# Latent query products: the rank of 448 cut as three row tiles of 128 and a stacked rest of 64, in place of four tiles of 112

## What is computed

```python
cq, ckv, k_rope, z = jnp.split(h @ w_in, [448, 960, 1024], axis=-1)
q = (rms_norm(cq, q_norm_g) @ w_uq).reshape(B, S, 16, 128 + 64)
kv = (rms_norm(ckv, kv_norm_g) @ w_ukv).reshape(B, S, 16, 128 + 128)
# rotary embedding on q_rope and k_rope, chunk-causal softmax, values
y = o.reshape(B, S, 2048) * jax.nn.silu(z)
return y @ w_out
```

## Time and profile before

| | us |
|---|---|
| median of 3 runs | 2478.34 (2477.54 to 2480.36) |
| the profiled execution | 2477.93, its span 2476.1 |
| PE busy | 2433.2 (98% of the span) |
| VectorE busy | 1889.0 (76%) |
| ScalarE busy | 1399.4 (57%) |
| GpSimd busy | 442.0 (18%) |
| granted TensorE clock, mean | 0.999 of full speed |

### The profile page before, as it was taken

The page is one execution under the profiler, slowest core; times in us unless marked ns, Lnnn a source line. Parts: engine busy times, 40 slices in busy tenths (PEclk is TensorE's granted clock), DMA queues, the critical chain, the costliest instruction groups (busy, mean ns, idle before and its releaser), DMA issues.

```text
span 2476.1 us, 31108 instructions
## 1 busy us (share of the span) xinstructions
PE 2433.2 (98%) x11597; PEld 2018.7 (82%) x11597; DVE 1889.0 (76%) x2295; ACT 1399.4 (57%) x1934; POOL 442.0 (18%) x298
## 2 busy tenths in 40 slices
PE   6999999999999999998999999999999999999999
PEld 5888888888887989887888888888888888888887
DVE  7899798977777787866655555557988878788884
ACT  6655765444447555555566676755655545555553
POOL 0264563111020000110000000043111021111111
PEclk9999999999999999999999999999999999999999
DMA  9999677978784877754555556455465555646454
GB/s 364 321 341 349 237 256 273 336 283 290 271 313 149 246 212 220 233 208 149 167 173 163 177 153 183 157 187 187 155 236 170 204 187 191 217 170 221 170 203 154
DMA packets 370999, 549.47 MB, mean 222 GB/s; under 512 B 31405, under 2 KB 158129, under 8 KB 370225
## 3 DMA queue, kind: packets, MB, share of 16 engines
q1 hardware_dynamic: 368688, 539.54, 64.6%
q10 hardware_dynamic: 1824, 6.04, 0.7%
q0 software_dynamic: 352, 2.11, 0.2%
HBM read 545.53 MB, written 2.11 MB: 221 GB/s over the span
## 4 chain that ended last, share of the span: by engine, by line
PE 88%; DVE 8%; ACT 2%; issue 1%; DMA 1%; SPq 0%; POOL 0%; DVEq 0%; ACTq 0%; POOLq 0%
PE ps L2393 48%; PE ps L2398 24%; DVE lo L1305 3%; PE ps L2423 2%; PE ps L2419 2%; PE ps L2420 2%; DVE ps L1330 1%; PE ps L2379 1%; PE ps L2378 1%; PE ps L2380 1%; DVE lo L1282 1%; DMA raw<-in_sgu_w_in 1%; PE ps L3007 1%; PE ps L2655 1%; ACT hi L630 1%
## 5 line engine op out<-in xcount | busy, mean ns | idle before, releaser
L1305 DVE TENSOR_TENSOR lo<-raw,hi 128x1024 fp32r<-128x1024 f32 x550 | 706.9, 1304 | 350.8 <-ACT hi L630 350.2
L630 ACT ACTIVATE hi<-raw 128x1024 fp32r<-128x1024 f32 x550 | 571.3, 1051 | 431.3 <-PE ps L2398 352.7
L2393 PE MATMUL ps<-hi,a_hi 128*128 128x512 f32 (+1 forms) x2016 | 798.6, 396 | 2.1 <-issue 0.9
L2393 PE MATMUL ps<-hi,a_lo 128*128 128x512 f32 (+1 forms) x2016 | 785.6, 390 | 0.0
L2398 PE MATMUL ps<-lo,a_hi 128*128 128x512 f32 (+1 forms) x2016 | 539.0, 389 | 1.5 <-DVE lo L1305 1.5
L616 ACT ACTIVATE hi<-raw 128x1024 fp32r<-128x1024 f32 x339 | 358.2, 1060 | 292.7 <-PE ps L2398 255.2
L1282 DVE TENSOR_TENSOR lo<-raw,hi 128x1024 fp32r<-128x1024 f32 x339 | 424.4, 1272 | 107.2 <-ACT hi L616 105.0
L2393 PEld LDWEIGHTS ps<-hi,a_hi 128*128 128x128 f32 x2016 | 378.7, 188 | 85.1 <-issue 5.3
L2398 PEld LDWEIGHTS ps<-lo,a_hi 128*128 128x128 f32 x2016 | 378.4, 188 | 81.1 <-DVE lo L1305 1.9
L2393 PEld LDWEIGHTS ps<-hi,a_lo 128*128 128x128 f32 x2016 | 378.9, 188 | 74.4
L2393 PE MATMUL ps<-hi,b_hi 128*128 128x512 f32 x880 | 347.4, 395 | 0.6 <-ACT y L1015 0.3
(11 more groups left out here) (351 smaller groups left out, 2436.6 us busy)
## 6 DMA issues: line engine op xcount, KB each, us to landing
raw<-in_sgu_w_in SPq DMA_DIRECT2D x88, 1024.0 KB
raw<-in_ada_w SPq DMA_DIRECT2D x64, 1024.0 KB
raw<-in_w_up SPq DMA_DIRECT2D x64, 1024.0 KB
raw<-in_w_down SPq DMA_DIRECT2D x64, 1024.0 KB
raw<-in_w_in SPq DMA_DIRECT2D x42, 1024.0 KB
raw<-in_ada_w SPq DMA_DIRECT2D x64, 512.0 KB
raw<-in_sgu_w_out SPq DMA_DIRECT2D x32, 1024.0 KB
raw<-in_w_in SPq DMA_DIRECT2D x128, 256.0 KB
```

The source lines that it names most:

```text
L630: nc.scalar.activation(hi[:, q % CHUNKS, 0:width], raw[:, r % RAWS, q % 2 * CW:q % 2 * CW + width], ACT.Copy).then_inc(hi_ready, 1)
L1305: nc.vector.tensor_tensor(lo[:, q % CHUNKS, 0:width], raw[:, r % RAWS, q % 2 * CW:q % 2 * CW + width], hi[:, q % CHUNKS, 0:width].bitcast( ...
L2393: nc.tensor.matmul(ps[:, 2 * s + t, 0:width], x[:, k0 + j, t * P:(t + 1) * P], hi[:, c, w], start=begins, stop=False)
```

## The change

The latent query is cut as three tiles of 128 rows and a rest of 64. The rest stands twice in tile 3: rows 0 to 63 of `b_hi` hold its high part, rows 64 to 127 its low part, and the weights' rest is loaded twice too, into both halves of the rows. One product of 128 rows with the weights' high part then gives two of the three terms, and a product of 64 rows, weights' low part by query's high part, the third: 3 x 3 + 2 = 11 products per output. For this VectorE writes the last 64 scaled columns twice, a fifth split operation goes to rows 64 to 127 of `b_hi`, the gain's rest is loaded twice, and an even head's weights come in 12 transfers, an odd head's in 3. `LAND` goes from 96 to 224 so that a slab can be divided into that many parts.

```diff
-LAND = 96
+LAND = 224
@@ the small vectors, SP
-                (rb[B_QG:B_QG + 4, 0:112], d["mla_q_norm_g"].rearrange("a (r q) -> (a r) q", q=112)),
+                (rb[B_QG:B_QG + 3, :], d["mla_q_norm_g"][:, 0:384].rearrange("a (r q) -> (a r) q", q=P)),
+                (rb[B_QG + 3:B_QG + 4, 0:64], d["mla_q_norm_g"][:, 384:448]),
+                (rb[B_QG + 3:B_QG + 4, 64:P], d["mla_q_norm_g"][:, 384:448]),
@@ head_parts, SP
-                    place = lambda c0, c1: lambda s: s[0:112, e * CW:(e + 1) * CW].rearrange("p (k n) -> p k n", k=4)[:, :, c0:c1]
-                    q0 = i * 192
+                    q0, wide = i * 192, P if i % 2 else S
+                    rows = lambda s, p0, p1, k0, k1: s[p0:p1, e * CW + k0 * wide:e * CW + k1 * wide]
+
+                    def placed(cut, source):
+                        return [(lambda s: cut(rows(s, 0, P, 0, 3).rearrange("p (k n) -> p k n", k=3)), source(uq_tiles))] + [
+                            (lambda s, p=p: cut(rows(s, p, p + 64, 3, 4).rearrange("p (k n) -> p k n", k=1)),
+                             source(uq_rest.rearrange("p (k n) -> p k n", k=1))) for p in (0, 64)]
+
                     if i % 2:
-                        return [(lambda s: s[0:112, e * CW:e * CW + NB].rearrange("p (k n) -> p k n", k=4), uq[:, :, q0:q0 + P])]
-                    return [(place(c, c + w), uq[:, :, q0 + q:q0 + q + w]) for c, w, q in
-                            ((0, 160, 0), (160, 32, 320), (192, 32, 160), (224, 32, 352))]
+                        return placed(lambda a: a, lambda w: w[:, :, q0:q0 + P])
+                    return placed(lambda a: a[:, :, 0:160], lambda w: w[:, :, q0:q0 + 160]) + placed(
+                        lambda a: a[:, :, 192:224], lambda w: w[:, :, q0 + 160:q0 + 192]) + placed(
+                        lambda a: a[:, :, 160:192], lambda w: w[:, :, q0 + 320:q0 + 352]) + placed(
+                        lambda a: a[:, :, 224:256], lambda w: w[:, :, q0 + 352:q0 + 384])
@@ ScalarE
-            act_split(act, n, 2, b_hi, 112, scale=lambda k: vb[0:112, B_QG + k:B_QG + k + 1], fresh=True)
+            act_split(act, n, 2, b_hi, scale=lambda k: vb[:, B_QG + k:B_QG + k + 1], fresh=True)
@@ VectorE
+        def dve_split_query(dve, n):
+
+            for g in range(2):
+                dve.wait_ge(t_hi, n.tg.base + 1)
+                for e in range(2):
+                    k = 2 * g + e
+                    for rows, to in ((slice(0, 64), b_lo), (slice(64, P), b_hi)) if k == 3 else ((slice(0, P), b_lo),):
+                        ins = nc.vector.scalar_tensor_tensor(out=to[rows, k, :], in0=ps[rows, 4 + n.tg.base % 2, e * S:(e + 1) * S],
+                                                             scalar=vb[rows, B_QG + k:B_QG + k + 1], in1=b_hi[rows, k, :].bitcast(F32),
+                                                             op0=ALU.mult, op1=ALU.subtract)
+                ins.then_inc(t_lo, 1)
+                n.tg.base += 1
@@
             dve_norm(dve, n, 448)
             for t in range(T):
+                nc.vector.tensor_scalar(v[:, t, D + 448:D + 512], cq[t][:, 384:448], rstd[:, t:t + 1], None, ALU.mult).then_inc(c_ready, 1)
+            dve.wait_ge(c_ready, 4)
+            for t in range(T):
                 nc.vector.tensor_scalar(cq[t], cq[t], rstd[:, t:t + 1], None, ALU.mult).then_inc(c_ready, 1)
@@
-            dve_split(dve, n, 2, b_hi, b_lo, 112, scale=lambda k: vb[0:112, B_QG + k:B_QG + k + 1])
+            dve_split_query(dve, n)
@@ PE
-            pe.wait_ge(small_landed, 128)
+            pe.wait_ge(small_landed, 160)
@@ query, PE
-                    for k in range(4):
+                    for k in range(3):
                         w = slice(k * step + q, k * step + q + P)
-                        ins = three(o, b_hi[0:112, k, :], b_lo[0:112, k, :], hi[0:112, c, w], lo[0:112, c, w], k == 0, k == 3, True)
+                        three(o, b_hi[:, k, :], b_lo[:, k, :], hi[:, c, w], lo[:, c, w], k == 0, False, True)
+                    w = slice(3 * step + q, 3 * step + q + P)
+                    mm(o, hi[:, c, w], b_hi[:, 3, :], start=False, stop=False)
+                    ins = mm(o, lo[0:64, c, w], b_hi[0:64, 3, :], start=False, stop=True)
@@
-            latent(4, lambda t, k: v[:, t, D + 112 * k:D + 112 * (k + 1)], 112)
+            latent(6, cols(v, D))
```

More of the change, by code:

```diff
@@ L530, in _ @@
                            LAND - 48 if q == 3 else 16) for q in range(4)))
-            uq = d["mla_w_uq"][0].rearrange("(k p) n -> p k n", p=112)
+            uq = d["mla_w_uq"][0]
+            uq_tiles = uq[0:3 * P, :].rearrange("(k p) n -> p k n", p=P)
+            uq_rest = uq[3 * P:448, :]
             ukv = d["mla_w_ukv"][0].rearrange("(k p) n -> p k n", p=P)
```

## The result

The changed kernel takes 2487.58 us (median of 8 runs, 2484.54 to 2490.19), the kernel before, run beside it on the same chip, 2480.61 (8 runs, 2477.54 to 2481.77): a ratio of 1.0027, 95% interval 1.0018 to 1.0037. It is slower, by 7.0 us. The profiled execution took 2487.03 us with a span of 2485.2; that of before had 2476.1, so between the two profiles lie 9.1 us.

A forecast was written before the change was run, and what follows sets the result against it. PE (TensorE) was taken to bound the kernel, with 88% of the chain. Profiled 2477.93 us + 6.0 for PE in the head loop + 0.75 for the opening, with the 0.4 to the median, gave 2485.0 us; range 2477.0 to 2488.0.

The forecast's parts named there:

- the base: Starting time of the forecast: the profiled execution's 2477.93 us, plus 0.4 because it lay that far below the median.
- The products removed: Head loop, latent query: 24 of 288 products go, 0.12 us each, 2.9 us less PE work.
- The 64-row product: Eleventh product of each output: going into 64 rows and out costs PE 0.40 us, bounded by 0 and 0.45.
- The first rival: The 64-row product costs no switch; half the saving is lost to VectorE's full stretches: 2477.6 us, chance 0.20.
- its half: The array must be freed but the 64-row product's weight load stays hidden, +0.08 us per output: 2480.3 us, chance 0.04.
- What PE's waits absorb: Heads 0, 4, 8, 12: PE's waits for the exponential hide 0.7 of 6.7 us, leaving +6.0 on the path.
- SP's queue: Head loop: 80 more weight transfers, even slabs issued 3.0 to 4.3 us later, landing 0.5 to 1.4 later; cost 0.
- PE's waits in heads 4, 8 and 12 gone: Sign expected in the changed trace: PE no longer waits for the exponential (L1032) in these heads.
- The second rival: The whole 3.8 us of later issue reaches the slabs of heads 6, 10, 14: 5.7 on top, 2490.7 us, chance 0.08.
- VectorE and ScalarE: Latent query: fifth split operation +0.41 us, norm scalings at most +0.8, ScalarE's extra rows free; nothing reaches PE.
- The opening: Kernel start: two more small-load issues on SP, ahead of ada_w's second slab, add 0.75 us that nothing makes up.
- The clock: Third rival: later PE loses or gains a lower-clock piece worth 3.5 us: 2481.5 or 2488.5 us, chance 0.04.

The follow-up runs named there:

- e1: The changed kernel with the eleventh product at all 128 rows in place of 64: 2481.84 us, ratio to before 1.0004.
- e2: The kernel before with only the last of an output's twelve products at 64 rows in place of 112: 2489.99 us, ratio 1.0034.
- e4: The changed kernel with the two 64-row products of an even head side by side (second form; the first gave no time): 2486.44 us, ratio 1.0020.
- e9: The changed kernel, 64-row product kept, with query weights loaded as before in 4 transfers and 1: 2487.91 us, ratio 1.0020.
- e8: The kernel before, unchanged, profiled once more as a control: 2482.66 us, ratio 1.0005.
- e12: The changed kernel with the eleventh product at 128 rows and the weights' rest loaded once (8 transfers and 2): 2480.69 us, ratio 0.9999.
- e5: The changed kernel with the eleventh product at 128 rows and query weights loaded as before (4 transfers and 1): 2481.58 us, ratio 0.9996.
- e11: As e10, and all nine small loads of the opening from ScalarE's queue: 2482.38 us, ratio to before 1.0004.
- e10: The changed kernel, eleventh product at 128 rows, both rest copies by one transfer (8 and 2), gain loaded from ScalarE's queue: 2481.97 us, ratio 1.0001.
- e6: The kernel before with the query norm's gain loaded in three pieces in place of one: 2481.41 us, ratio 0.9999.
- e3: The changed kernel with the eleventh product at 96 rows in place of 64: 2482.22 us, ratio to before 1.0007.
- e7: The kernel before with query weights in 12 transfers (even heads) and 3 (odd) in place of 4 and 1, products unchanged: 2482.05 us, ratio 1.0003.

## Why the prediction was right, and where it wasn't

**Forecast and base.** 2485.0 us was said and 2487.58 measured, inside the range, slower as said. The difference was put at 6.7 us over the median shown, and 7.0 was measured. 2.3 of the 2.6 us of the miss are the base: the three runs shown had a median of 2478.34, later ones of the same kernel 2480.6 to 2481.8.

**The products removed** cost 0.12 us each, as said; 24 are gone.

**The 64-row product** costs 0.38 us in and out per output, against 0.40 from the attention scores of the second block. The mechanism read there, time until the array is free and a weight load that nothing hides, is what the timeline of after shows (the 64-row product starts 0.09 us late and the next one 0.19, each with its load beside it, and the one after that 0.10), and it carries over to products of the other precision with one half of the rows. e1 and e2 show it from both sides, e4 that it is the step that costs. Per output it is + 0.26 and not + 0.28. The first rival (2477.6) fell with e1 and e2, and its half too.

**What PE's waits absorb** was put at 0.7 us. In e9, with the loads of before, the loop has 21 x 0.26 = 5.46 us more PE work and is 5.04 longer: 0.4 absorbed; ahead of it 3 x 0.26 = 0.78 and 0.47 longer: 0.3. Together 0.7, and e9's trace has no wait for the exponential left. So 24 outputs at + 0.26 less the 0.7 are 5.5 us on the path, where + 6.0 was said.

**SP's queue** was put at nothing; it is 1.0 us (e9 against after). This is the mis-sized term, and it made up for the 0.5 above; that the forecast came so near is in this part luck. The step that failed is the length of the later issue: at 0.32 to 0.5 us a transfer it was 3.0 to 4.3 us; the twelve took 8.15 us in place of 2.18, 6.0 more. Of the 5.2 us behind the last issue, in which it was to lie, 1.4 are still there in after, so only 3.8 of the 6.0 were covered. Counted from the first issue, ScalarE got the slabs of heads 6, 10 and 14 2.1, 1.8 and 2.8 us later than before, and not 0.5 to 1.4; in hand were 1.1 and, with PE slower, 0.8 more. PE's waits come in the same order: 0.1 us in head 4, none in head 8, 0.4 in head 12, so that "PE's waits in heads 4, 8 and 12 gone" holds for head 8 alone. ScalarE's waits are 1.7 us longer per slab than in before, 1.2 than in e8. The second rival's mechanism was at work, at a sixth of its price of 5.7. e12 shows that the reasoning as such holds up to 5.5 us of issue.

**VectorE and ScalarE** at nothing: in e1, e5 and e11, which have the fifth split and the second scaling, the stretch to turn 0 is 112.47 to 112.48 us, as in the control's 112.48.

**The opening** at + 0.75: the mean start of the first product moved by 0.67. That nothing behind makes it up wasn't shown. If all of it reaches the end, the parts are 5.5 + 1.0 + 0.7 = 7.2 us, where the medians differ by 7.0; medians of this kernel can't tell that from 6.5. The reason given, the second slab issued later, can't be the whole of it, since e11 issues that slab 4 us earlier and gains nothing.

**The saving that can't be had.** The first rival said that without a row step only half of the 2.9 us would come out, 1.4, since VectorE sets the end in heads 0, 4, 8 and 12. e5 and e12 have just that, 1.5 us in the loop, the first with the weights' old transfers and the second without the second copy of their rest. So even with transfers that cost nothing this change is worth less than what a measurement of this kernel can tell.

**The clock** rival: after had a piece at the lower level that before had not, worth 1.1 us in that one profile (114.08 against e9's 112.95). Two variants with the eleventh product at 128 rows (e10, e12) had such a piece too, and e9, with 64 rows, had none there, so it isn't the change's alone. The price of the rival was too high. The piece behind the head loop lasts 6.8 us in before and 3.4 in e6 and e12 (granted clock 0.97 between 1100 and 1150 us), but their last stretch of the table isn't shorter by 1.7 us: 1438.23 and 1438.43, against 1438.29 and 1438.40. PE is busy for only 41.32 of the 50 us there, so it doesn't set the time.

## What to carry to other kernels

One product fewer isn't a gain if one of those left steps down to 64 rows: the step into 64 rows and out costs as much as three of these 256-column products. Either give that product all the rows, if what it then adds does no harm, or put the 64-row products of several outputs side by side, which pays the step once. Before counting a saving on PE, look which engine sets the end in each part of the loop, and before splitting a load, compare the time in which the queue issues a whole slab with the time in hand; and judge edits of one stage by marks inside the profile, which here repeated to 0.1 us while whole runs of one kernel scatter by 4 to 10.

## What the runs showed of the hardware

Of the row counts tried, 64 costs a step between products with 128 rows, and 96 doesn't (e3). The Trainium skill, TensorEngine Tiling (Array Packing), Key Properties, says that a change of the tiling mode drains the TensorE, which fits 0.38 us at 64 rows and nothing at 96. It isn't the rows alone: in the kernel before, products with 128 rows and weights of 64 columns (L2916, 128*64) cost a step too. The chain there:

```profile
1217.27 0.81 PE ps L2916 x12
1218.07 2.04 PE ps L2393 x8
```

The block of eight behind them takes 2.04 us, as behind 64 rows (2.05), and not 1.83 as behind transposes of 128 by 128.

The scatter of this kernel isn't spread over the run: against before, ScalarE's high parts shift only in the first 335 us, and from there to the 251st (738 us in before) each variant keeps its distance or comes back to it. One source is at the very start. The first products of 512 columns in before:

```profile
29.51 0.47 PE L2393 MATMUL ps<-hi,a_hi 128*128 128x512 f32 x1 [0.94 <-issue]
29.81 0.39 PE L2393 MATMUL ps<-hi,a_lo 128*128 128x512 f32 x1
```

and in e8_control, the same kernel:

```profile
29.77 0.77 PE L2393 MATMUL ps<-hi,a_hi 128*128 128x512 f32 x1 [0.95 <-issue]
30.34 0.63 PE L2393 MATMUL ps<-hi,a_lo 128*128 128x512 f32 x1
30.76 0.63 PE L2393 MATMUL ps<-hi,a_hi 128*128 128x512 f32 x1
```

In the second the products last 0.63 us and start 0.42 apart, and not 0.39 and 0.23. The granted clock of the profile is 1.00 there in both kernels (29.5 to 34 us). But the pace is that of the piece near 780 us in after, where the granted clock is at the lower of its two levels (1.2 GHz; 0.62 of full speed in the window at the end, which holds 3.4 us of it):

```profile
782.29 0.63 PE L2571 MATMUL ps<-hi,a_hi 128*128 128x512 f32 x1
782.72 0.63 PE L2572 MATMUL ps<-hi,a_lo 128*128 128x512 f32 x1
```

So e8 probably starts at the lower level too; that the clock record misses it isn't shown. By ScalarE's 13th high part e8 is 2.4 us behind, 0.3 of it from the start. At 161 us it is 3.1 us behind, and most of the rest comes from there to 203 us. Between 160 and 215 us ScalarE waits 19.9 us for slabs of `sgu_w_in` in e8 and 15.7 in before; the longest of these waits in e8 ends at 203.46:

```profile
203.46 1.06 ACT L630 ACTIVATE hi<-raw 128x1024 fp32r<-128x1024 f32 x1 [4.20 <-DMA raw<-in_sgu_w_in]
```

Why the slabs come later there isn't shown. In other kernels the shift comes later: e7 falls 3.5 us back and e5 5.3 between 264 and 333 us.

The piece at the lower clock near 780 us in after, in a window of 4.5 us (columns as in the earlier trace rows):

```profile
780.00:784.50 4.50, 4.50 (x17) 3.44 (x16) 1.65 (x4) 2.11 (x6) 0.00 (x0) 0.62 0.44 169
```

Before has 1.00 in the same window.
